# A two-layer diffusion trunk on one core: a new order for the first loads and norm, for the query and key items, and for the convolution's layer norm

## The reference, cut to what matters

```
h = rms_norm(x) * (1 + scale) + shift      # scale, shift, gate from silu(cond) @ ada_w + ada_b
z = h @ w_in                               # 1024 -> 1024 (conv a|b) + 512 (q) + 128 (k) + 128 (v)
g = a * sigmoid(b)
y = depthwise_conv(g, 31 taps) + dw_b      # context and latent are separate sequences
conv = silu(layer_norm(y) * ln_g + ln_b)   # over the 512 channels
q, k = rms_norm per head (latent: with rotary)
att = softmax(q k^T / 8) v                 # 8 heads, 2 key heads; latent also sees cached keys
x = x + gate1 * (concat(conv, att) @ w_out)
```

## Time and profile before

| what | value |
|---|---|
| median of three runs | 1418.31 us (1417.85 to 1419.4) |
| span of the profiled execution, first to last instruction | 1415.6 us |
| its own device time | not recorded apart; the median of the runs lies 2.7 us above the span |
| PE busy | 1275.7 us, 90% of the span |
| DVE, ACT, POOL busy | 903.4, 772.1, 285.1 us |
| mean granted TensorE clock | 0.935 of 2.4 GHz |

### The profile page before, as it was taken

How to read it: one execution, slowest core, us unless ns; L and a number is a source line. 1 busy time by engine, 2 the same in 40 slices (tenths; PEclk the granted TensorE clock), 3 DMA queues, 4 the chain that set the end, 5 groups by cost and what they waited for, 6 DMA issues and landing times.

```text
span 1415.6 us, 19778 instructions
## 1 busy us (share of the span) xinstructions
PE 1275.7 (90%) x7731; PEld 1122.0 (79%) x7731; DVE 903.4 (64%) x1165; ACT 772.1 (55%) x1118; POOL 285.1 (20%) x236
## 2 busy tenths in 40 slices
PE   5896899899999998986967898999999999999895
PEld 3794566799889987984655697889989889889793
DVE  1448856453434345656575624889789799799776
ACT  3467664542323225324556424677777777777673
POOL 0367850200110012000003021012312303213113
PEclk9998998899999999996985896999999999999998
DMA  9842993243443254412921121699899899899882
GB/s 307 227 145 86 299 332 106 76 152 109 141 138 116 97 164 141 136 61 67 311 77 60 31 82 47 204 333 336 268 348 316 281 337 324 281 341 321 278 284 86
DMA packets 178362, 277.68 MB, mean 196 GB/s; under 512 B 7121, under 2 KB 105193, under 8 KB 178265
## 3 DMA queue, kind: packets, MB, share of 16 engines
q1 hardware_dynamic: 176040, 269.87, 57.6%
q0 software_dynamic: 2224, 6.49, 1.7%
HBM read 274.02 MB, written 2.31 MB: 195 GB/s over the span
## 4 chain that ended last, share of the span: by engine, by line
PE 70%; DVE 12%; issue 9%; ACT 5%; DMA 2%; POOL 1%; SPq 1%; DVEq 0%; ACTq 0%; POOLq 0%
PE psB L1963 5%; PE psB L1965 5%; PE psB L1964 5%; PE psB L1473 4%; PE psB L1475 4%; PE psB L1474 4%; PE psA L1963 3%; PE psA L1965 3%; PE psA L1964 3%; DVE Wl L2583 2%; PE psB L1703 2%; PE psB L1701 2%; PE psB L1702 2%; PE psA L1914 2%; PE psA L1473 2%
## 5 line engine op out<-in xcount | busy, mean ns | idle before, releaser
L2583 DVE TENSOR_TENSOR Wl<-raw,Wh 128x1408 fp32r<-128x1408 f32 (+2 forms) x144 | 247.2, 1740 | 58.1 <-ACT Wh L1373 57.1
L2026 DVE TENSOR_TENSOR Wl<-raw,Wh 128x2048 fp32r<-128x2048 f32 (+4 forms) x64 | 133.8, 2096 | 143.8 <-ACT Wh L1015 143.5
L1373 ACT CAST Wh<-raw 128x1408 fp32r<-128x1408 f32 (+2 forms) x144 | 196.9, 1374 | 27.6 <-PE psA L1965 14.4
L1015 ACT CAST Wh<-raw 128x2048 fp32r<-128x2048 f32 (+4 forms) x64 | 110.0, 1724 | 118.1 <-PE psB L1703 64.2
L1963 PE MATMUL psA<-Wh,hTh 128*128 128x352 f32 x360 | 118.3, 329 | 0.7 <-ACT hTl L1379 0.7
L1965 PE MATMUL psA<-Wh,hTl 128*128 128x352 f32 x360 | 116.6, 324 | 0.0
L1964 PE MATMUL psA<-Wl,hTh 128*128 128x352 f32 x360 | 116.0, 322 | 0.0
L920 POOL TENSOR_TENSOR yc<-yc,work 128x414 f32<-128x414 f32 x90 | 100.9, 1143 | 54.3 <-ACT work L1114 51.7
L1473 PE MATMUL psB<-Wh,hTh 128*128 128x256 f32 (+2 forms) x356 | 105.4, 296 | 7.0 <-DVE Wl L2026 2.5
L1474 PE MATMUL psB<-Wl,hTh 128*128 128x256 f32 (+2 forms) x356 | 104.7, 294 | 0.0
L1475 PE MATMUL psB<-Wh,hTl 128*128 128x256 f32 (+2 forms) x356 | 104.6, 294 | 0.0
(11 more groups left out here) (375 smaller groups left out, 3396.6 us busy)
## 6 DMA issues: line engine op xcount, KB each, us to landing
raw<-in_l_moe_w SPq DMA_DIRECT2D x108, 704.0 KB, 5.3
raw<-in_l_ada_w SPq DMA_DIRECT2D x48, 1024.0 KB, 5.8
raw<-in_l_ffn_w SPq DMA_DIRECT2D x28, 1024.0 KB, 5.3
raw<-in_l_moe_w SPq DMA_DIRECT2D x27, 768.0 KB, 6.3
gate_b<-in_l_moe_w SPq DMA_DIRECT2D x18, 768.0 KB, 6.9
gate_b<-in_l_moe_w SPq DMA_DIRECT2D x18, 704.0 KB, 5.7
raw_tail<-in_l_moe_w SPq DMA_DIRECT2D x18, 704.0 KB, 5.6
raw<-in_l_w_in SPq DMA_DIRECT2D x11, 1024.0 KB, 5.5
```

The source lines that it names most:

```text
L1015: act.copy(hi_of(u), raw_of(u)).then_inc(hi_ready, 1)
L1373: act.copy(half_of(Wh, h), raw_half(h)).then_inc(half_hi, 1)
L2026: dve.tensor_tensor(lo_of(u), raw_of(u), hi_of(u).bitcast(F32), ALU.subtract).then_inc(lo_ready, 1)
L2583: dve.tensor_tensor(half_of(Wl, h), raw_half(h), half_of(Wh, h).bitcast(F32), ALU.subtract).then_inc(half_lo, 1)
```

## The change

1. **Front.** Blocks 0 to 7 get four places of their own (`front_raw`, in memory that is free until the first norm is done), and units alone use the raw places. SP issues blocks 3 to 7 as their places come free, unit 0 behind block 5, then units 1 to 4. PE does block 7 in its turn, and all of convolution unit 0 behind the last two turnings, with the last spread behind two of its eight parts.
2. **Small loads.** The 13 gains, four caches and four gate biases of layer 0 are issued by SP, behind unit 4 and ahead of unit 5, instead of by POOL.
3. **Items.** The squares of tiles 0 and 1 are made at once, the three items follow each other, and both gated values come behind item 2.
4. **Taps.** ACT makes three taps in every attention step until they are used up.
5. **Layer norm.** `average(0)` stands in attention step `LN_AT` = 22, the subtraction behind it, and the squares in step 23. `average(1)` follows the attention.
6. **Output.** PE does two tiles of `out_part(0, 0)` ahead of the turning of the last tile of heads. ACT and DVE split unit `ou + 1` there, and `ou + 2` only when the SiLU is done.

```diff
-        order = ([("block", d) for d in range(FRONT - 2)] + [("unit", 0)] +
-                 [("block", d) for d in range(FRONT - 2, FRONT)] + [("unit", u) for u in range(1, base["out", 0])] +
+        order = ([("unit", u) for u in range(base["out", 0])] +
...
-            load_in_order(0, RING)
+            for d in range(3):
+                load_block(d)
...
-            load_in_order(RING, len(order))
+            load_block(3)
+            for d in range(FRONT_PLACES, FRONT):
+                sp.wait_ge(aside_used, d - FRONT_PLACES + 1)
+                load_block(d)
+                if d == 5:
+                    load_in_order(0, 1)
+            load_in_order(1, SMALL_LOADS)
+            sp.wait_ge(psT_full, 2)
+            sp.wait_ge(spread_full, FRONT)
+            for name, view in G.items():
+                sp.dma_start(view, A[name].partition_broadcast(P)).then_inc(gains_in, 16)
...
+            for gate in range(2):
+                for c in range(2):
+                    src = A["l0_ada_b"][(3 * gate + 2) * D:(3 * gate + 3) * D]
+                    sp.dma_start(gate_b[:, gate, c, :], src.partition_broadcast(P)).then_inc(gate_bias_in[0], 16)
+            load_in_order(SMALL_LOADS, len(order))
...
@@ ACT, attention
-                        for _ in range(3 if s < 9 else 2):
+                        for _ in range(3):
                             tap()
@@ ACT, items
+            act.wait_ge(psB_free, qkv_group(QKV0 - 1, NT - 1) + 1)
+            squares(0, 0)
+            squares(0, 1)
             for j in range(NT):
-                act.wait_ge(psB_free, qkv_group(QKV0 - 1, NT - 1) + 1)
-                squares(0, j)
                 qk_root(HD, 10)
-                if AHEAD_CONV + j < CT:
-                    table_of(ACT.Sigmoid)
-                    gate_of(AHEAD_CONV + j)
+                if j == 0:
+                    squares(0, 2)
                 for _ in range(4):
                     tap()
+            table_of(ACT.Sigmoid)
+            for n in range(AHEAD_CONV, CT):
+                gate_of(n)
...
             attend(0)
-            split_to(ou + 2)
+            split_to(ou + 1)
@@ PE, attention
+                    if a == 0 and i == LN_AT:
+                        average(0)
+                if a > 0:
+                    o_transpose(a, NT - 1)
@@ PE, front
             for d in range(FRONT):
-                if d == FRONT - 1:
-                    for k in range(4):
-                        pe.wait_ge(hT_lo, H["norm0"] + k + 1)
-                        conv_products(k)
                 aside_product(d)
...
-            front_spread(FRONT - 1)
-            for k in range(4, KD):
+            for k in range(KD):
+                if k == 2:
+                    front_spread(FRONT - 1)
@@ PE, output
-            average(0)
+            average(1)
             pe.wait_ge(spread_free, LATE_0)
+            pe.wait_ge(hT_lo, H["att0"] + NT - 1)
+            out_part(0, 0, (0, 1))
+            o_transpose(0, NT - 1)
             pe.wait_ge(hT_lo, H["att0"] + NT)
-            out_part(0, 0, (0, 1))
-            average(1)
             out_part(0, 0, (2,))
@@ DVE, attention and items
+                    if a == 0 and i == LN_AT:
+                        centred()
+                    if a == 0 and i == LN_AT + 1:
+                        squared()
+                if a == 0:
+                    variance_out()
                 o_low(a, NT - 1)
...
-                if AHEAD_CONV + j < CT:
-                    gated_value(AHEAD_CONV + j)
+            for n in range(AHEAD_CONV, CT):
+                gated_value(n)
```

More of the change, by code:

```diff
@@ L46 @@
 RING = 3
+SMALL_LOADS = 5
 S = 3
@@ L375, in trunk_step @@
         mods_ready = sem("mods_ready")
-        gate_bias_in = sem("gate_bias_in")
+        gate_bias_in = [sem(f"gate_bias_in{l}") for l in range(2)]
         c_in, c_turned = sem("c_in"), sem("c_turned")
         aside_landed = [sem(f"aside_landed{i}") for i in range(RING)]
+        front_landed = [sem(f"front_landed{i}") for i in range(FRONT_PLACES)]
         aside_used = sem("aside_used")
@@ L518, in tgroup, with lngroup @@
         def tgroup(a, s):
-            return first[f"attend{a}"]["T"] + s + sum(otile_at(t) <= s for t in range(NT - 1))
+            return first[f"attend{a}"]["T"] + s + sum(otile_at(t) <= s for t in range(NT - 1)) + (a == 0 and LN_AT <= s)
         def otgroup(a, t):
             f = first[f"attend{a}"]["T"]
-            return f + otile_at(t) + t if t < NT - 1 else f + 8 * NT + NT - 1
+            return f + otile_at(t) + t if t < NT - 1 else f + 8 * NT + NT - 1 + 2 * (a == 0)
+        def lngroup(n):
+            return first["attend0"]["T"] + (8 * NT + NT if n else LN_AT + NT - 1)
         def ckvT(h):
@@ L880, in _, with gate_bias @@
         def _(pool):
[L881 to L887, removed]
+            def gate_bias():
                 for gate in range(2):
                     for c in range(2):
-                        src = A[f"l{l}_ada_b"][(3 * gate + 2) * D:(3 * gate + 3) * D]
-                        pool.dma_start(gate_b[:, gate, c, :], src.partition_broadcast(P)).then_inc(gate_bias_in, 16)
+                        src = A["l1_ada_b"][(3 * gate + 2) * D:(3 * gate + 3) * D]
+                        pool.dma_start(gate_b[:, gate, c, :], src.partition_broadcast(P)).then_inc(gate_bias_in[1], 16)
             def add(b):
@@ L1658, in average @@
             def average(n):
-                g = first["lnorm"]["T"] + n
-                pe.wait_ge(ln_in, n + 1)
+                g = lngroup(n)
+                if n == 0:
+                    pe.wait_ge(conv_chain, CW)
+                    pe.wait_ge(conv_chain_p, adds_before(len(p_taps)))
+                else:
+                    pe.wait_ge(ln_in, 1)
                 free_t(g)
@@ L2151, in columns_out, with centred, squared, variance_out @@
                 dve.tensor_copy(dst, psB[g % 3][:, first_col:n]).then_inc(psB_free, 1)
+            def centred():
+                g = lngroup(0)
+                dve.wait_ge(psT_full, g + 1)
+                for c in range(CT):
+                    ins = dve.tensor_tensor(yc[:, c, :], yc[:, c, :], psT[g % 2][:, 0:COUT], ALU.subtract)
+                    if c < CT - 1:
+                        link(ins)
+                ins.then_inc(psT_free, 1)
+                dve.wait_ge(psT_free, g + 1)
+            def squared():
+                for c in range(CT):
+                    ins = dve.tensor_tensor(cpad[:, c, 0:COUT], yc[:, c, :], yc[:, c, :], ALU.mult)
+                    if c < CT - 1:
+                        link(ins)
+                ins.then_inc(ln_in, 1)
+            def variance_out():
+                g = lngroup(1)
+                dve.wait_ge(psT_full, g + 1)
+                link(dve.tensor_copy(hf[:, 0, 0:P], psT[g % 2][:, 0:P]))
+                dve.tensor_copy(hf[:, 0, P:TOK], psT[g % 2][:, 2 * PAD + P:COUT]).then_inc(psT_free, 1)
+                dve.wait_ge(psT_free, g + 1)
             taps = [0]
```

63 lines of the change are left out of this document (24 added, 39 removed).

## The result

The changed kernel took 1429.66 us (median of 4 runs, 1429.01 to 1433.56), the kernel before 1418.19 beside it. The forecast was 1418.7 within 1411 to 1425, so it was wrong.

The account below looks back on a forecast made before the run. TensorE, busy 90% of the span, was taken as the bound, with its idling and lower clock in the first 260 us in question. Terms -6.3 + 4.0 + 0.4 + 2.3 = +0.4 us gave 1418.7 us, range 1411 to 1425.

Parts of the forecast that it names:

- The front: Start to the end of the queries: they end at 90.5 instead of 96.8 us, 6.3 us earlier.
- the twelve matmuls ahead of the last spread: In the front, two parts of the convolution: 12 matmuls at 0.32 us, the spacing at the lower clock.
- the pause of 2.5 us: PE's wait for a weight split between convolution unit 1 and the queries, claimed to go.
- Small loads: 21 loads on SP's queue between units 4 and 5: claimed to cost nothing, by half a microsecond to two.
- The limit of 77: Latest landing of unit 5, in us, without PE waiting in the query units; landing was expected near 75 to 76.5.
- Rival (b): Query units: unit 5 lands after 77 us and PE stops, losing 5 us if it takes 16: 1423.7; chance 0.27.
- The rule that I weighed: DMA engines alternate between queues but work one ring in order, putting unit 5 wholly behind the 21 loads: the slow rival.
- Items: End of the queries to first exponential: +36.3 us instead of +32.3, 4.0 us later; bounds +1.0 and +5.5.
- Rival (a): Items keep their gain and the clock does not fall again in the output: -4.6 us, 1413.7; chance 0.35.
- Taps: Attention steps with three POOL adds per step to the end: 0.4 us later, bounds 0 and 2.
- Layer norm and output: Average to the start of the convolution's half (r = 1): 2.3 us later; ends 0.3 and 4.5.
- Two falls of the clock: In layer norm and output, PE dropping to the lower clock twice: 4.5 us later, the slow end of that term.

Follow-up runs that it names:

- items_alone: The kernel before with only the items and gated values in the new order; ratio to before 1.0023, +3.3 us.
- behind_unit6: The changed kernel with all 21 small loads behind unit 6 on SP's queue; +7.4 us (5.0 to 9.9) against the kernel before.
- pool_queue: The changed kernel with all 21 small loads back on POOL's queue, behind the clearing of cpad; +4.8 us (2.7 to 6.8) against the kernel before.

## Why the prediction was wrong

**The front: right in size by luck, lost on the way.** Without the pause it brings 6.2 us over the means (forecast 6.3). Two errors of some 3 us cancel in that. The queries ended at 87.2 instead of 90.5, because convolution unit 1 started 3.4 us earlier than I let it; 1.8 of that are the twelve matmuls ahead of the last spread, which ran 0.17 us apart, at full clock, and not 0.32. And the trace of before that I subtracted from had a front 2.9 us above the mean of six; the pause of 2.5 us that I saw the change remove is small in most other traces of the old front.

**Small loads: this is the step that failed.** "So it costs nothing by half a microsecond to two": it cost the 6 us of the pause. The greater fault is the due time. The limit of 77 was counted back from 81.6, from my late start of the projections; PE stopped at 78.3, so the load was due by 73.7 (less 0.4, 2.3 and 1.9). The better the front, the earlier the load is due: I had worked the gain and the limit out as if they were independent. The landing was off by less, 77.8 and not 75 to 76.5. Unit 5 was issued at 65.9, near the 65 that I had, but only because two errors met: unit 4 was issued at 52.4 and not at 56, and the 21 loads behind it took 13.0 us to issue (52.9 to 65.9) where I had 9; 4.54 of them are the four gate biases, for which I had 1.6.

Rival (b) named the place and the wait and put it at 5 us; its chance was 0.27, and as a sum (+5.4) it explains half of the loss. That its 5 us are near the 6 is luck: they came from a landing at 82 (16 us from an issue at 66), and the load took 11.9 us.

The rule that I weighed (the Trainium skill, "DMA: Bandwidth & Descriptors", section "Queues, rings and completion order") had spoken against the change, and the trace agrees: behind the gate biases in one ring unit 5 landed at 77.8, after the last of them (74.5), beside them on another queue at 72.2. The two differ in the time of issue as well, by 10.3 us, and no run here parts the order in the ring from the order of the issues.

**Items: right.** Forecast +4.0, measured +3.3 over the traces and by `items_alone` alike, with 25.0 and 26.4 us for items and gated values and 35.9 for 36.3. The last agreement is in part luck: the terms that I listed behind the gated values add up to 37.3 to 37.8, not to 36.3; they were too long in all, 10.9 to 11.4 us for a stretch that took 9.4. Rival (a), in which they keep the gain, is out.

**Taps: small.** Forecast 0.4, measured +1.1 over the traces, but the old order's spread (45.4 to 50.6) is wider than that, and by itself the edit is +0.6 (-1.8 to 2.8). What size it has stays open.

**Layer norm and output: the mechanism right, the term mis-sized.** Forecast +2.3 with 4.5 as its end, measured +5.6 over the means (5.0 between the two single traces). From the last minimum to the last value product's end it takes 12.5 instead of 6.7 us, +5.8 (forecast 5.2). Behind it I wanted 27.0 us to r = 1, and it took 29.1 (27.9 to 29.3 in five traces). The second average was taken at 2.5 us from the price at full clock. It took 4.3 to 5.9 in all nine traces that have the new layer norm, wholly or partly at 0.50, with a wait of PE of 1.0 to 5.2 us just ahead of it or ahead of the last value product. The new order moved the slow average and did not spare it: in the old order the first one took 4.5 to 5.9 and the second 2.9 to 3.1, in all eight traces. The start of r = 1 at 0.50 adds 1.1. "Two falls of the clock" stood only as an end of the range; they are the usual case.

**The third attention: not the change.** In the single pair of traces it looks like half of the loss. It is a difference between executions, shown by the kernel before itself. The near agreement of the difference of the spans (11.6 us) with the measured one (10.8) is chance: the trace of before was 2.9 us above its mean in the front, which hides a loss, and 3 to 6 us below the other traces in the third attention, which feigns one. The forecast was counted from that same trace.

So the forecast of +0.4 misses by 10.4: 6.0 from the pause, 3.3 from the layer norm, 0.7 from the taps, less 0.7 that the items cost under their forecast, and the rest, 1.1, is within what the runs can tell.

## What to carry to other kernels

When an edit makes a stage start earlier, count every load that the stage needs back from the new start, not from the old: the due times move by as much as the gain. Loads that can wait belong on another queue or behind those that can't, and what stands ahead of an urgent load is to be counted by its bytes and by how long it takes to issue, not by its number: four loads of 512 KB held SP's queue for 4.54 us, the 13 gains for 6.2. Before a profile's differences are explained one by one, take a second trace of the unchanged kernel: stretches may differ by several microseconds with no cause in the code, and a pause that the first trace shows may be absent from the second.

## What had not been expected of the hardware

The four broadcasts of 512 KB took 4.54 us to issue on SP's queue (3.5 to 5.5 in the five other traces with the same order, 3.74 in `behind_unit6`), over 1 us each in the mean, while the 13 gains took some 0.43 each. It is not shown that the broadcast makes them slow. The first two took 0.5 us each and the last two 2.0 and 1.4; two ordinary halves of weight units behind them, also of 512 KB, took 4.19 and 3.25, and one in `pool_queue` took 7.80, where others took 0.37. On POOL's queue the same four took 2.12 us in `pool_queue`, but the four of layer 1 took 3.51 in the kernel before. The long issues on SP's queue came while other loads were in flight; what sets their length stays open.

The granted clock of one unchanged kernel has its low stretches in different places from one execution to the next. Between two traces whose spans differ by 0.9 us, that moves the third attention by 6 us and the front by 1.4, and a load that lands 3 us sooner or later moves the front by 3 more. PE at 0.50 looks busier than PE at 1.00 (15.00 and 14.87 of 15 us against 13.07 in the windows shown, at a clock of 0.50 and 0.55 against 1.00): a busy share alone hides it, the count of matmuls doesn't.
